# Seven block products instead of eight in the input projection of a hybrid attention layer, and a second value tensor for the shared heads

## The reference, cut to what matters

```
proj = x @ w_in                       # (4096, 1024) @ (1024, 3328), float32
aq, ak, av, ag, bq, bk, bv, bg = split(proj)   # 512 x 4, 512, 128, 128, 512 columns
ya = chunk_relbias_attention(aq, ak, av, rel_bias) * silu(ag)   # 8 heads, 9 chunks of 64
qb, kb = partial_rope(bq), partial_rope(bk)                     # 16 of 64 columns turned
yb = sliding_window_sink_gqa(qb, kb, bv, sinks) * silu(bg)      # 8 query heads, 2 shared key/value heads
mix = concat([ya, yb]) @ w_out
h = 2 ** 0.25 * x + mix
h = h + sigmoid(h @ w_gate) * (p @ w_ple)
out = layer_norm(h) * ln_g + ln_b
```

## Time and profile before

| what | us |
|---|---|
| median of 3 runs | 2696.57 |
| lowest, highest | 2695.4, 2698.49 |
| the profiled execution's own time | 2700.69 |
| its span, first to last instruction | 2698.9 |
| first stage, until TensorE's first matmul of attention A | 1168.96 |
| TensorE busy | 2584.9 |
| VectorE busy | 1215.2 |
| ScalarE busy | 1002.7 |
| GpSimd busy | 354.6 |

### The profile page before, as it was taken

The page is one execution under the profiler, slowest core; times in us unless marked ns, Lnnn a source line. Parts: engine busy times, 40 slices in busy tenths (PEclk is TensorE's granted clock), DMA queues, the critical chain, the costliest instruction groups (busy, mean ns, idle before and its releaser), DMA issues. The chain is left out here.

```text
span 2698.9 us, 38010 instructions
## 1 busy us (share of the span) xinstructions
PE 2584.9 (96%) x14100; PEld 2257.2 (84%) x14100; DVE 1215.2 (45%) x2433; ACT 1002.7 (37%) x2091; POOL 354.6 (13%) x192
## 2 busy tenths in 40 slices
PE   7999999999999999999999999977999999999997
PEld 5888888998888888999989898875788888888886
DVE  5212136341111165158878786875433334334333
ACT  4111112231111122158878787764322322322222
POOL 2000000000000000000000000001344343443442
PEclk9999999999999999999999998998999999999999
DMA  6432237373322165385556547786444444444440
GB/s 198 150 119 75 82 88 136 134 239 119 131 86 82 62 120 150 121 280 162 167 170 215 167 127 241 249 226 183 111 118 108 131 116 109 120 120 117 118 111 34
DMA packets 365482, 377.06 MB, mean 140 GB/s; under 512 B 81560, under 2 KB 290600, under 8 KB 361640
## 3 DMA queue, kind: packets, MB, share of 16 engines
q1 hardware_dynamic: 364456, 374.61, 47.2%
q0 software_dynamic: 896, 0.80, 0.1%
HBM read 240.33 MB, written 136.07 MB: 139 GB/s over the span
## 5 line engine op out<-in xcount | busy, mean ns | idle before, releaser
L1345 PE MATMUL psum<-x_hi,w_hi 128*128 128x512 f32 x1344 | 525.1, 391 | 19.7 <-DVE x_lo L1049 17.5
L1345 PE MATMUL psum<-x_lo,w_hi 128*128 128x512 f32 x1344 | 525.1, 391 | 0.0
L1345 PE MATMUL psum<-x_hi,w_lo 128*128 128x512 f32 x1344 | 524.8, 390 | 0.0
L1345 PEld LDWEIGHTS psum<-x_hi,w_hi 128*128 128x128 f32 x1344 | 253.2, 188 | 72.6 <-issue 17.5
L1345 PEld LDWEIGHTS psum<-x_hi,w_lo 128*128 128x128 f32 x1344 | 253.2, 188 | 52.8
L1345 PEld LDWEIGHTS psum<-x_lo,w_hi 128*128 128x128 f32 x1344 | 253.1, 188 | 52.3
L722 POOL TENSOR_TENSOR y_raw<-y_two 128x512 f32<-128x512 f32 x32 | 41.2, 1286 | 1778.4 <-DMA y_two<-ya_d 1778.4
L1146 DVE CUSTOM_DVE_ANT_0 prob<-psum,bias 128x640 f32<-128x640 f32 (+4 forms) x256 | 199.2, 778 | 90.4 <-issue 90.0
L854 ACT ACTIVATE prob<-prob,small 128x640 f32<-128x640 f32 (+4 forms) x256 | 203.9, 797 | 65.2 <-DVE small L1146 61.1
L1243 DVE TENSOR_TENSOR y_lo<-y_raw,y_hi 128x1024 fp32r<-128x1024 f32 x32 | 39.2, 1225 | 397.6 <-ACT y_hi L883 397.6
L1345 PE MATMUL psum<-wo_hi,y_hi 128*128 128x512 f32 x512 | 203.2, 397 | 1.5 <-DVE wo_lo L1238 1.5
(11 more groups left out here) (163 smaller groups left out, 4854.0 us busy)
## 6 DMA issues: line engine op xcount, KB each, us to landing
qk_d<-stage_out SPq DMA_DIRECT2D x72, 512.0 KB, 2.7
w_raw<-in_w_in SPq DMA_DIRECT2D x20, 1024.0 KB, 5.5
v_d<-stage_out SPq DMA_DIRECT2D x64, 320.0 KB, 2.3
x_raw<-in_xT SPq DMA_DIRECT2D x32, 512.0 KB, 4.8
g_d<-stage_out SPq DMA_DIRECT2D x64, 256.0 KB, 2.0
bq_d<-stage_out SPq DMA_DIRECT2D x64, 256.0 KB, 4.1
ya_d<-y_a SPq DMA_DIRECT2D x128, 128.0 KB, 2.6
bq<-bq_d SPq DMA_DIRECT2D x32, 512.0 KB, 5.8
```

The lines of the kernel that those rows point to most:

```text
L1345: return pe.matmul(dst, lhs, rhs, start=start, stop=stop)
```

## The change

**The products.** The summed dimension (1024) is cut into two halves, the columns are taken in pairs of 128-column blocks, and the tokens in pairs of 512. This makes a 2 by 2 by 2 product of blocks, which needs eight block products when it is written out, and which the changed kernel computes with seven, by a scheme with sums and differences of blocks of x (`T1` to `T4`, `D2`), of blocks of the weights (`mix_weights`), and of the results (`combine`). The stage has four groups of 1024 tokens. In each come ten pairs of column blocks (`PAIRS`, two of them, numbers 3 and 7, hold rotated queries), each with seven products of 12 matmuls of 128x512; then the values (four steps `m`), which stay with all their products; then the rotated keys (four products of 12 matmuls).

**Who does the sums.** GpSimd makes four differences or sums of 128x512 for the weights of each pair, and from the second group on also `T3`, `T2`, `T1`, `D2` (two halves of 128x1024 each). VectorE makes `T4`, and all of them in the first group, and the seven results' sums of a pair. ScalarE takes two copies (`snapshot`) out of PSUM per pair. Low and high parts are made once for each of the seven weight blocks of a pair, five ahead of TensorE, in a ring of seven.

**The values of the two shared heads** go to `bv_d`, ordered by head, token in chunk, chunk. Each `load_bv` is then two DMAs of 64 partitions, in each of which a partition reads one run of up to 16 KB. The store of them is two more DMAs with pieces of 512 bytes.

**The host** now hands over x and the weights in blocks (`x_blocks`, `w_blocks`, `w_values`). The SBUF map of the first stage is new, and the order of `pt_lo` and `bias` in attention A is swapped.

```diff
-            for half in range(2):
-                def unit(number, bank, slot, c, j):
-                    pe.wait_ge(acc_free, number + 1)
-                    for k in range(KT):
-                        mm(psum[:, bank, :], wh, xh, k == 0, False)
-                        mm(psum[:, bank, :], wh, xl, False, False)
-                        last = mm(psum[:, bank, :], wl, xh, False, k == KT - 1)
+            for g in range(GROUPS):
+                for a in range(BK):
+                    base = 3 * (a % 2)
+                    for i in range(7):
+                        if i == 0 and a >= 2:
+                            pe.wait_ge(unit_done, unit(g, "q", a - 2, 3) + 1)
+                        if i == 2:
+                            pe.wait_ge(snap_done, snapped(g, "q", a, 0) + 1)
+                        if i == 4:
+                            pe.wait_ge(sum_done, summed(g, "q", a, "U2") + 1)
+                        if i == 5:
+                            pe.wait_ge(snap_done, snapped(g, "q", a, 1) + 1)
+                        if i == 6:
+                            pe.wait_ge(sum_done, summed(g, "q", a, "U3") + 1)
+                        pe.wait_ge(w_split, ring(g, a, i) + 1)
+                        if a == 0:
+                            pe.wait_ge(x_split, x_at(g, X_OF[i]) + 2)
+                        feature_product(base + (0, 1, 0, 2, 0, 2, 0)[i], ring(g, a, i), X_OF[i])
```

The order of the x blocks in the seven products is `X_OF = ("X11", "X21", "T2", "T1", "T3", "X22", "T4")`. VectorE's part, inside the loops over group g, pair a and product i:

```diff
+                        if a == 0 and i == 1 and g > 0:
+                            rope_unit(unit(g - 1, "k", 1), 10 * g - 1, 1, snap[:, 4, :])
+                        for name in ((), ("C11",), ("U2",), (), ("U3", "U4", "C22"), ("C12",), ("C21",))[i]:
+                            combine(g, a, name)
+                        if a < BK - 1 or i < 4:
+                            w_lo(ring(g, a, i) + W_AHEAD)
+                        if a == 0 and i == 0 and g > 0:
+                            dve.wait_ge(sum_done, summed(g - 1, "k", 1) + 1)
+                            rope_unit(unit(g - 1, "k", 0), 10 * g - 2, 0, snap[:, 3, :])
+                            x_block(g, "T4")
+                        if i in (1, 4, 5):
+                            pair_out(g, a, (1, 4, 5).index(i))
+                        if i == 6:
+                            pair_out(g, a, 3)
```

ScalarE's part, inside the same loops, and what it does between two groups:

```diff
+                        if i in (0, 3):
+                            snapshot(g, a, i // 3)
+                        if a < BK - 1 or i < 4:
+                            w_hi(ring(g, a, i) + W_AHEAD)
+                        rope = PAIRS[a][0] == "bq"
+                        if i in ((2, 5, 6) if rope else (1, 4, 5)):
+                            pair_out(g, a, ((2, 5, 6) if rope else (1, 4, 5)).index(i))
+                        if i == 6:
+                            pair_out(g, a, 3)
...
+                    for name in ("X11", "T3", "T2", "X21", "T1", "X22"):
+                        x_block_hi(g + 1, name)
```

GpSimd's queue, and the load of the shared values on SyncE's:

```diff
+            mix_weights(0, 0)
+            mix_weights(0, 1)
             pool.wait_ge(setup, 3)
             for g in range(8):
                 for c in range(2):
                     pool.dma_start(trig_d[c, :, TB * g:TB * g + TB], swap[16 * g:16 * g + 16, c, :]
                                    ).then_inc(setup_stored, 16)
+            for g in range(GROUPS):
+                for a in range(2 if g == 0 else 1, BK):
+                    mix_weights(g, a)
+                if g + 1 < GROUPS:
+                    mix_weights(g + 1, 0)
+                    for name in ("T3", "T2", "T1", "D2"):
+                        for part in range(2):
+                            x_combine(pool, g + 1, name, part)
...
-                sp.dma_start(v_b[:, s, n0:B_HALF // CHUNK, :].bitcast(f32),
-                             bass.AP(tensor=v_d.tensor, offset=first,
-                                     ap=[[row, P], [CHUNK * row, B_HALF // CHUNK - n0], [1, P]])
+                sp.dma_start(v_b[0:CHUNK, s, skip:count, :].bitcast(f32), bv_d[kv, :, first + skip - 1:first + count - 1, :]
+                             ).then_inc(bv_loaded[s], 16)
+                sp.dma_start(v_b[CHUNK:P, s, :, :].bitcast(f32), bv_d[kv, :, first:first + count, :]
                              ).then_inc(bv_loaded[s], 16)
```

More of the change, by code:

```diff
@@ L57, with prod, unit, snapped @@
 STRIPS = 13
-X_CHUNKS = 4 * JB
-X_RING = 3
 ALPHA32 = float(np.float32(ALPHA))
+def prod(g, kind, a=0, b=0):
+    return 98 * g + {"q": 7 * a + b, "v": 70 + 6 * a + b, "k": 94 + a}[kind]
+def unit(g, kind, a=0, b=0):
+    return 58 * g + {"q": 4 * a + b, "v": 40 + 4 * a + b, "k": 56 + a}[kind]
+def snapped(g, kind, a=0, b=0):
+    return 29 * g + {"q": 2 * a + b, "v": 20 + 2 * a + b, "k": 28}[kind]
+def summed(g, kind, a=0, b=0):
+    return 88 * g + {"q": 7 * a + ("C11", "U2", "U3", "U4", "C22", "C12", "C21").index(b) if kind == "q" else 0,
+                     "v": 70 + 4 * a + (b if kind == "v" else 0), "k": 86 + a}[kind]
+def ring(g, a, i):
+    return 72 * g + 7 * a + i
+def ring_read(n):
+    g, r = divmod(n, 72)
+    return prod(g, "k", (1, 3)[r - 70]) if r >= 70 else prod(g, "q", r // 7, r % 7)
+def x_at(g, name):
+    order = ("X11", "X21", "X22", "T3", "T2", "T1", "T4") if g == 0 else ("X11", "T3", "T2", "X21", "T1", "X22", "T4")
+    return 14 * g + 2 * order.index(name)
+def stored_before(u):
+    def stores(v):
+        v %= 58
+        if v < 40:
+            return 2 if PAIRS[v // 4][0] == "bq" else 1
+        return 3 if v < 56 and v % 2 == 1 else 1
+    return sum(16 * stores(v) for v in range(u % 2, u, 2))
 def b_unit(u):
@@ L145, in build, with v_raw @@
+        X_OF = ("X11", "X21", "T2", "T1", "T3", "X22", "T4")
+        def v_raw(k):
+            return v_raw_a[:, k, :] if k < 6 else v_raw_b[:, k - 6, :]
         aq_hi, aq_lo = (sb(n, [P, 2, SEQ], f32r) for n in ("aq_hi", "aq_lo"))
```

938 lines of the change are left out of this document (579 added, 359 removed).

## The result

The changed kernel takes 2864.2 us (median of 4 runs, 2860.6 to 2867.6) against 2696.5 us beside it on the same chip: a ratio of 1.062, with a 95% interval from 1.060 to 1.064. It is 168 us slower. The forecast was 2780 us, 83 us slower, with a range up to 2830: the direction was right, the size half of what came, and the time lies outside the range.

What follows compares the result with a forecast made beforehand. The prediction took the first stage as bound by TensorE; -108.6 us for removed matmuls and +61, +48, +15, +7, +9, +26, +30, -4 made +83 on 2700.7, so 2784, with the median at 2780, range 2640 to 2830.

Steps and rivals of the forecast that it cites:

- Removed products, -108.6: First stage, column pairs: 480 fewer matmuls at 0.226 us each, nothing hiding the gain, -108.6 us.
- Rotated pairs +61: Eight rotated query pairs: TensorE waits 0.9 us inside and 6.7 us behind each for late VectorE and ScalarE, +61 us.
- gaps +48: Three changes of token group: TensorE waits 15.9 us each for new x blocks, snapshots and U2, +48 us.
- start and set-up +15: First group: an earlier first product, then waits for x sums and U2, and rotation tables delaying weight sums, +15 us.
- Values, +7: End of each group's pairs: the last value weights are ready 1.8 us late, four times, +7 us.
- GpSimd beside VectorE: First stage: GpSimd's reads block VectorE's SBUF operations, taken at +30 us between nothing and full turns.
- upper end of 57: GpSimd and VectorE taking turns: 3 x 12 in gaps, 8 x 2 in rotated pairs, 5 at the start, 57 us.
- The clock: First stage: half clock behind 13 long stalls loses 21 to 42 us of work, taken at +26 us.
- `v_b`, -4: Attention B: larger load pieces shorten at most two stalls and their clock, 0 to -8, taken at -4 us.
- Into attention A, +9: Start of attention A: the second score waits for VectorE's two rotated key units, 20 against 11 us, +9 us.
- Rival (c): Full turns of GpSimd and VectorE plus the clock's upper bound: +27 and +16, 2823 us; chance 0.15.
- Rival (a): Seven products pay because VectorE and ScalarE keep ahead of TensorE: 2640 us named; chance 0.2.

Runs made afterwards that it cites:

- e3_pool_fill: The changed kernel with GpSimd writing zeros where it made sums of weight and x blocks, so that it reads nothing: 2800.7 us.
- e13_short_xsums: The changed kernel with each of GpSimd's sums of x blocks for the next group cut into two of 128x512: 2854.2 us.
- e5_filler: The changed kernel with 24 added matmuls in the pair behind each rotated pair, into the bank of the waiting product 2: 2837.3 us.
- e6_rotated_late: The changed kernel with VectorE rotating only behind the sums that products wait for, ScalarE and SyncE reordered to follow: 2838.9 us.
- e7_gap_order: The changed kernel with T4 and the second rotated key unit put behind U2 between groups: 2858.3 us.
- e1_old_values: The changed kernel with the shared heads' values back in the ten-head tensor, stored and loaded as before: 2851.9 us.
- e11_before_new_values: The kernel before with only the new values tensor, its three stores and two loads: 2708.8 us against 2700.5 us, ratio 1.0036.

## Why the prediction was wrong

The forecast was that the first stage would do 108.6 us of matmuls less and lose more than that in waits. That held. By its own steps, the sum of +83 against the +160 of the spans:

- **Removed products, -108.6.** Right: 3360 matmuls for the pairs, 1136 to 1027 us of work.
- **Rotated pairs +61, gaps +48, start and set-up +15.** Right as a map of the queues. Without GpSimd's reads (`e3_pool_fill`) the rotated pairs lose 8 x 7.2 = 57.5, the gaps 3 x 13.3 = 40 (the two small waits of 1.6 and 1.2 us per gap did not come), and the start's two large waits are within 0.4 us.
- **Values, +7: too low.** In `e3_pool_fill` the value weights cost 4 x 2.4 and the value snapshots another 14.9. I had looked at TensorE's wait for the weights, and not at ScalarE, whose snapshots stand in its queue behind the value results. This is +17.
- **GpSimd beside VectorE, "I take +30": the step that failed first.** Its measured value is 63.5, above even the upper end of 57 that took turns of the two engines everywhere. The discount ("part falls where VectorE idles") was not earned: the bunched stretches of VectorE are those that TensorE waits for, and the x sums stand in one of them. By place, the waits of the changed kernel less those of `e3_pool_fill` are 34 us in the gaps (the upper end had 36), 11 in and behind the rotated pairs (16), and 5 in the first pairs of the start (5). So where the upper end looked, it was near. What lies above it stands where the prediction gave blocking no term at all: 10 us at the value weights and 4 in pair 2 of the first group (a wait of 10.4 us instead of 6.0). The rule of the Trainium skill, "SBUF — State Buffer", section "Who interferes with whom", that the prediction quoted, agrees with the 1.63 us row above, where VectorE ended 0.54 us behind GpSimd's sum; of a sum that is itself slowed it gives the order of issue as the cause, and GpSimd's 2.2 us halves in `e13_short_xsums` fit that.
- **The clock, "+26", for 13 stalls: the second.** The loss grew by 55 us. The price of a wait was low (2.0 taken, 2.4 in `e5_filler`), and above all the count was wrong. Behind the start the stage has 21 waits of 3.3 us and more, and by the distances between matmuls behind each of them they cost 1.6 to 3.2 us of clock, 2.5 on average and 53 in all. The 19 shorter ones (0.5 to 2.4 us) cost 0.2 to 0.4 each. The eight that I had not counted are the first wait of each gap (8.7), the one of 10.4 us in pair 2, and four among the values (4.06, 3.29, 3.30, 6.49): 18 us of the 29 that were missing. Nine more are the price of the 13 (35 us instead of 26). `e6_rotated_late` and `e7_gap_order` show why the count matters: waits of 3.6 us cost 1.7 to 3.6 us of clock, those of 15 to 16 us 2.4 to 3.1.
- **`v_b`, -4: wrong in sign.** It is +7.6 in attention B with the seven products (`e1_old_values`) and +5.4 with the eight (`e11_before_new_values`), while the loads arrive at 229 to 235 GB/s in place of 308 to 312; which property of them makes it so is not shown.
- **Into attention A, +9.** Right: the wait is 8.9 us, and the stage 6.8 longer.

The errors are +33.5 for GpSimd, +29 for the clock, +17 for the values, +11 for `v_b`, -8 for the gaps and some -6 for the rest, together the 77 us that are missing. Rival (c), full turns and the clock's upper bound, had the two failed terms in it and named 2823: its mechanism was the right one, still 41 us short. Rival (a) falls for every order tried: even with all orders changed and no sums on GpSimd (2706.3) the seven products do not beat the eight. What a schedule with fewer weight sums could do (each is made four times, once per group) was not tried.

## What to carry to other kernels

Work taken from a saturated TensorE pays only if the engines that prepare its operands have room at each point where it waits for them, not on average: here VectorE had the room over a group, and TensorE waited 223 us. Count each wait twice, for its length and for the stretch at half clock behind it, and do not cut a long wait into several of 4 us. If the preparation is shared by VectorE and GpSimd with operands in SBUF, price both as one engine wherever they are active together, and look for such places through the whole stage, not only where the queue is longest.

## What the hardware showed that I had not expected

- GpSimd and VectorE slow each other both ways: a VectorE 128x1024 subtraction of 1.22 us took 2.96 on average and a GpSimd sum of 2.39 took 3.37 in the gaps between groups. With GpSimd writing zeros and reading nothing, the subtraction took 1.22 again.
- Behind the waits of 3.60, 7.42 and 15.36 us shown above TensorE's clock was at 1.2 GHz, for some 5 us of full work. Behind a wait of 2.36 us for the value weights, which ended at 274.76, it was still at 2.4 GHz:

```profile
274.00:278.00 4.00, 3.24 (x22) 3.27 (x23) 3.30 (x5) 2.30 (x5) 0.94 (x1) 1.00 0.85 304
282.00:286.00 4.00, 3.43 (x15) 3.43 (x16) 0.98 (x2) 0.00 (x0) 1.65 (x1) 0.68 0.59 212
```

  The second window follows a wait of 4.06 us that ended at 282.57. But the length of a short wait does not decide it. The same wait in `e3_pool_fill`, as long, left the clock at 1.2 GHz, and so did one of 1.96 us in the first stage before:

```profile
261.36 0.39 PE L1617 MATMUL psum<-vw_hi,xs_hi_a 128*128 128x320 f32 x1 [2.35 <-DVE vw_lo L1210]
263.00:265.00 2.00, 2.00 (x10) 2.00 (x9) 1.30 (x3) 1.69 (x3) 0.45 (x1) 0.50 0.73 272
...
1054.68 0.42 PE L1345 MATMUL psum<-w_hi,x_hi 128*128 128x320 f32 x1 [1.96 <-DVE w_lo L1002]
1056.00:1058.00 2.00, 2.00 (x10) 2.00 (x9) 1.29 (x2) 0.64 (x2) 0.00 (x0) 0.50 0.81 240
```

  What else decides it, no run here tells.
- Runs of up to 16 KB on 64 partitions moved a quarter less per second than 512-byte pieces on 128 partitions, with the DMA engines fully busy in both.
